# 512-column products in four more kinds of stage, weights stored in blocks, and a convolution tap on ScalarE

## What is computed

```
# block 1
h = rms_norm(x, pre_mix_g);  z = h @ w_in                      # 2048 x 4096: q, k, v, u
m = concat(chunked_attention(q, k, v), multiscale_pool(u)) @ w_o   # "mixer output"
x = x + rms_norm(m, post_mix_g)
h = rms_norm(x, pre_ffn_g)
up = causal_dwconv(h @ w_up, conv_w, conv_b)                   # 3 taps along the sequence
y = (gelu(up[:, :5632]) * up[:, 5632:]) @ w_down               # down projection
x = x + rms_norm(y, post_ffn_g)
# block 2: adaptive norms from 64 column blocks of w_ada, two attentions, a gated merge, a SwiGLU
kv = modulate(norm(ctx and x)) @ w_in_2[:, :3072];  q = modulate(norm(x)) @ w_in_2[:, 3072:6144]
gates = modulate(norm(x)) @ w_in_2[:, 6144:]
x = x + gate * ((sigmoid(ga) * (oa @ w_br_a) + sigmoid(gb) * (ob @ w_br_b)) @ w_out)
x = x + gate * ((silu(h @ w_ff_gate) * (h @ w_ff_up)) @ w_ff_down)
```

## Time and profile before

| | |
|---|---|
| median of 3 runs | 3146.78 us (3143.88 to 3147.21) |
| the profiled execution | 3145.76 us |
| its span, first to last instruction | 3143.9 us |
| mean granted TensorE clock | 0.970 |
| TensorE busy | 2926.2 us (93%) |
| VectorE / ScalarE / GpSimd busy | 1946.6 / 1564.1 / 786.3 us |
| HBM read | 594.99 MB, 190 GB/s over the span |

### The profile page before, as it was taken

One profiled execution on the slowest core, in us unless ns is written; L12 is line 12 of the kernel. 1 busy time (PEld: TensorE's weight loads), 2 busy tenths in 40 slices (PEclk: granted clock), 3 DMA queues, 4 the chain that ended last, 5 costly groups with the idle time before them and its releaser, 6 DMA issues.

```text
span 3143.9 us, 57610 instructions
## 1 busy us (share of the span) xinstructions
PE 2926.2 (93%) x20282; PEld 2699.2 (86%) x20282; DVE 1946.6 (62%) x2412; ACT 1564.1 (50%) x2203; POOL 786.3 (25%) x646
## 2 busy tenths in 40 slices
PE   7998789999998997999998778999997999999999
PEld 7988789999988997788898547999996888888888
DVE  5566888776688866433456555655766665555554
ACT  5555554345565543323455645665535644334443
POOL 2554432003233321212341402445303400000000
PEclk9999899999999998999998989999998999999999
DMA  7874666657777764344574003887755865656655
GB/s 245 266 246 126 222 201 201 180 181 243 240 225 227 235 218 148 120 149 135 180 248 140 1 1 125 255 261 247 241 182 178 255 213 181 188 186 187 187 185 163
DMA packets 595176, 598.29 MB, mean 190 GB/s; under 512 B 18257, under 2 KB 593105, under 8 KB 594833
## 3 DMA queue, kind: packets, MB, share of 16 engines
q1 hardware_dynamic: 591936, 589.37, 60.3%
q10 hardware_dynamic: 2368, 4.91, 0.4%
q0 software_dynamic: 784, 2.88, 0.3%
HBM read 594.99 MB, written 2.10 MB: 190 GB/s over the span
## 4 chain that ended last, share of the span: by engine, by line
PE 60%; DVE 15%; DMA 10%; ACT 7%; issue 7%; DVEq 1%; ACTq 0%; SPq 0%
PE acc L1334 19%; PE acc L1330 13%; PE acc L1332 13%; PE acc L1333 12%; DVE wlo L850 5%; DMA raw<-w_ada 5%; DMA raw<-w_in 2%; ACT whi L540 2%; ACT cond_products L536 1%; DVE cond_sums L842 1%; DVE conv_out L936 1%; PE sums L1392 1%; DMA raw<-w_up 1%; DMA raw<-w_brb 1%; DVE conv_in L924 1%
## 5 line engine op out<-in xcount | busy, mean ns | idle before, releaser
L850 DVE TENSOR_TENSOR wlo<-raw,whi 128x1024 fp32r<-128x1024 f32 x864 | 1120.3, 1307 | 892.5 <-ACT whi L540 888.9
L1334 PE MATMUL acc<-operand,wlo 128*128 128x256 f32 (+1 forms) x5504 | 1606.6, 292 | 0.0
L540 ACT ACTIVATE whi<-raw 128x1024 fp32r<-128x1024 f32 x864 | 911.3, 1058 | 1096.5 <-PE acc L1334 733.5
L1332 PE MATMUL acc<-operand,whi 128*128 128x256 f32 (+1 forms) x4096 | 1222.6, 298 | 98.3 <-DVE wlo L850 63.4
L1333 PE MATMUL acc<-operand,whi 128*128 128x256 f32 (+1 forms) x4096 | 1210.7, 296 | 0.0
L1334 PEld LDWEIGHTS acc<-operand,wlo 128*128 128x128 f32 x5504 | 1063.0, 193 | 15.4
L1332 PEld LDWEIGHTS acc<-operand,whi 128*128 128x128 f32 x4096 | 795.4, 194 | 125.4 <-DVE wlo L850 56.5
L1333 PEld LDWEIGHTS acc<-operand,whi 128*128 128x128 f32 x4096 | 795.6, 194 | 15.0
L408 POOL TENSOR_TENSOR cond_products<-cond_products 128x512 f32<-128x512 f32 x192 | 252.6, 1316 | 1425.9 <-ACT cond_products L536 1424.0
L1330 PE MATMUL acc<-operand,whi 128*128 128x512 f32 x1408 | 502.9, 402 | 16.9 <-DVE wlo L850 9.0
L536 ACT ACTIVATE cond_products<-raw,cond_silu 128x256 f32<-128x256 f32 x768 | 327.8, 498 | 255.7 <-PE acc L1334 159.3
(11 more groups left out here) (201 smaller groups left out, 2000.0 us busy)
## 6 DMA issues: line engine op xcount, KB each, us to landing
raw<-w_ada SPq DMA_DIRECT2D x256, 512.0 KB, 4.7
raw<-w_in SPq DMA_DIRECT2D x224, 512.0 KB, 4.8
raw<-w_up SPq DMA_DIRECT2D x176, 512.0 KB, 4.8
raw<-w_down SPq DMA_DIRECT2D x88, 512.0 KB, 4.9
raw<-w_fg SPq DMA_DIRECT2D x88, 512.0 KB, 4.3
raw<-w_fu SPq DMA_DIRECT2D x88, 512.0 KB, 4.5
raw<-w_fd SPq DMA_DIRECT2D x88, 512.0 KB, 3.5
raw<-w_o SPq DMA_DIRECT2D x32, 512.0 KB, 4.8
```

Of the source, the lines that this page charges most:

```text
L540: act.activation(whi[j % RING][:], raw[j % RING][:], ACT.Copy).then_inc(hi_done, 2 if st.entries[j % st.upb - 1] == (None, ADA_VEC) else 1)
L850: dve.tensor_tensor(wlo[j % RING][:], raw[j % RING][:], whi[j % RING][:].bitcast(F32), ALU.subtract).then_inc(lo_done, 2 if prev[0] is Non ...
L1332: pe.matmul(out_, h[:, x, f], mov[:, 0], start=first, stop=False)
L1334: ins = pe.matmul(out_, l[:, x, f], mov[:, 0], start=False, stop=last)
```

## The change

- **Block layout.** Each of the eleven weight matrices is rearranged on the host to [partition, column block, row tile, 256 columns]; a unit is then 128 rows of 4 KB, one for each partition. For a partition the distance to the next is a 128th of the matrix, 128 KB (w_o) to 768 KB (w_ada).
- **512-column products** in kinds mix_out, down1, down2 and q too. In three of them (LOW_FIRST) ScalarE first copies the low half's sums from PSUM to the result tile (`low_half`), and VectorE's evacuation, which now comes after `lo`, adds the other half instead of copying. In down2 VectorE adds both halves.
- **Convolution.** VectorE's `evac` keeps only L924. The newest tap with the bias is made by ScalarE (`newest_tap`, two ACTIVATE Identity, right behind the `hi` of that step). VectorE makes the older taps in a function of its own, after `lo`: for the first group after the `lo` of the next ring entry, for the second after the `lo` of the same step, ahead of `finish`.

```diff
-V_STEPS = {"scale": 0, "mix_out": 3, "conv": (6, 9), "down1": 0, "down2": 3, "kv": 0, "q": 0, "gate": 0,
+V_STEPS = {"scale": 0, "mix_out": 3, "conv": (4, 7), "down1": 0, "down2": 4, "kv": 0, "q": 0, "gate": 0,
            "branch_a": 0, "branch_b": 1, "out": 4, "glu": (0, 3), "down_x": 3}
-A_STEPS = {"conv": (1, 0), "gate": (1, 1), "glu": (2, 1)}
-WIDE = ("glu", "down_x")
+A_STEPS = {"conv": (2, 1), "gate": (1, 1), "glu": (2, 1), "mix_out": 1, "down1": 1, "q": 1}
+WIDE = ("glu", "down_x", "mix_out", "down1", "down2", "q")
+LOW_FIRST = ("mix_out", "down1", "q")
...
+    def block_of(w, g, k):
+        return W[w][:, ds(g, 1), k:k + UK, :].rearrange("p g k c -> p (g k) c")
     def cols(w, k, c0, stride):
-        return lambda b, GB, gb, u: W[w][:, k + UK * u:k + UK * u + UK, ds((b * GB + gb) * stride + c0, GW)]
+        return lambda b, GB, gb, u: block_of(w, (b * GB + gb) * (stride // GW) + c0 // GW, k + UK * u)
...
...
             def post(st, b, gb):
                 g = group(st, b, gb)
-                if st.kind == "conv" and gb % 2 == 0:
+                if st.kind == "conv":
                     act.wait_ge(evac_done, g + 3)
                     act.activation(Gb[:], Cb[:], ACT.Gelu_apprx_tanh).then_inc(astep, 1)
...
+            def low_half(st, b, gb):
+                tile = b * (2 * st.GB) + (st.tile0 + 2 * gb)
+                act.wait_ge(used, grouped(st, b, gb))
+                act.activation(R[:, ds(tile if st.kind == "q" else tile + Yt, 2), :], PS[:, gb % 2, :, S:2 * S],
+                               ACT.Copy).then_inc(astep, 1)
...
+            def newest_tap(st, b, gb):
+                act.wait_ge(vstep, vst(st, b, gb, 0))
+                t2 = b * 2 + (FT * (gb % 2) + st.feat0 + VEC["conv_w"] + 4 * FT)
+                tb = b * 2 + (FT * (gb % 2) + st.feat0 + VEC["conv_b"])
+                for m in range(2):
+                    ins = act.activation(Cb[:, m, :], Zp[:, m, 2:S + 2], ACT.Identity, scale=V[:, ds(t2 + m, 1)],
+                                         bias=V[:, ds(tb + m, 1)])
+                ins.then_inc(astep, 1)
...
-                    at = j - RING - (2 if st.kind == "conv" else 0)
-                    if at in st.last:
+                    at = j - RING
+                    if st.kind == "conv":
+                        if at in st.last:
+                            newest_tap(st, b, st.last.index(at))
+                        elif at - 2 == st.last[0]:
+                            post(st, b, 0)
+                    elif at in st.last and st.kind in LOW_FIRST:
+                        low_half(st, b, st.last.index(at))
+                    elif at in st.last:
                         post(st, b, st.last.index(at))
...
-                if k == "q":
-                    dve.tensor_copy(R[:, ds(tile, 2), :], sums).then_inc(evac_done, 1)
-                elif k == "down1":
-                    dve.tensor_copy(R[:, ds(tile + Yt, 2), :], sums).then_inc(evac_done, 1)
+                if k in ("q", "down1"):
+                    y = R[:, ds(tile + Yt if k == "down1" else tile, 2), :]
+                    dve.wait_ge(astep, ast(st, b, gb, 0))
+                    dve.tensor_tensor(y, sums, y, ALU.add).then_inc(evac_done, 1)
...
                 elif k == "mix_out":
                     y = R[:, ds(tile + Yt, 2), :]
-                    did(dve.tensor_copy(y, sums))
+                    dve.wait_ge(astep, ast(st, b, gb, 0))
+                    did(dve.tensor_tensor(y, sums, y, ALU.add))
...
                         did(dve.tensor_tensor(y, y, sums, ALU.add))
+                        settled()
+                        did(dve.tensor_tensor(y, y, low, ALU.add))
...
                         did(dve.tensor_tensor(Zp[:, :, 2:S + 2], sums, rep(RS[:], 2), ALU.mult))
-                        settled()
...
-                        if gb % 2:
-                            dve.wait_ge(astep, ast(st, b, 0, 0))
-                        for m in range(2):
-                            did(dve.tensor_scalar(Cb[:, m, :], Zp[:, m, 2:S + 2], V[:, ds(t0 + (4 * FT + m), 1)],
-                                                  V[:, ds(tb + m, 1)], ALU.mult, ALU.add))
...
+            def older_taps(st, b, gb):
+                did, settled = steps_from(st, b, gb, 1)
+                settled()
+                dve.wait_ge(astep, ast(st, b, gb, 0))
+                t0 = b * 2 + (FT * (gb % 2) + st.feat0 + VEC["conv_w"])
+                for tap in (1, 0):
+                    for m in range(2):
+                        if tap == 0:
+                            settled(2)
+                        ins = dve.scalar_tensor_tensor(
+                            out=Cb[:, m, :], in0=Zp[:, m, tap:S + tap], scalar=V[:, ds(t0 + (2 * FT * tap + m), 1)],
+                            in1=Cb[:, m, :], op0=ALU.mult, op1=ALU.add)
...
-                    gate = st.kind in ("gate", "glu")
+                    gate = st.kind in ("gate", "glu", *LOW_FIRST)
...
                     if gb is not None and gate:
                         evac(st, b, gb)
+                    if st.kind == "conv" and gb != 0 and (gb == 1 or j - RING == st.last[0] + 1):
+                        older_taps(st, b, gb or 0)
                     if gb is not None:
                         finish(st, b, gb)
...
+    by_block = lambda w: np.ascontiguousarray(
+        w.reshape(w.shape[0] // P, P, w.shape[1] // GW, GW).transpose(1, 2, 0, 3))
...
-        "w_o": a["w_o"][0], "w_up": a["w_up"][0], "w_down": a["w_down"][0], "w_ada": a["w_ada_2"][0],
+        "w_o": by_block(a["w_o"][0]), "w_up": by_block(a["w_up"][0]), "w_down": by_block(a["w_down"][0]),
...
```

More of the change, by code:

```diff
@@ L125, in build @@
           w_fg, w_fu, w_fd, out):
-    km = lambda w: w.rearrange("(k p) n -> p k n", p=P)
-    W = {k: km(v) for k, v in dict(w_in=w_in, w_o=w_o, w_up=w_up, w_down=w_down, w_in2=w_in2, bra=w_bra, brb=w_brb,
-                                   out=w_out2, fg=w_fg, fu=w_fu, fd=w_fd).items()}
-    ada_src = km(w_ada)
+    W = dict(w_in=w_in, w_o=w_o, w_up=w_up, w_down=w_down, w_in2=w_in2, bra=w_bra, brb=w_brb, out=w_out2, fg=w_fg,
+             fu=w_fu, fd=w_fd, ada=w_ada)
+    def block_of(w, g, k):
+        return W[w][:, ds(g, 1), k:k + UK, :].rearrange("p g k c -> p (g k) c")
     def cols(w, k, c0, stride):
-        return lambda b, GB, gb, u: W[w][:, k + UK * u:k + UK * u + UK, ds((b * GB + gb) * stride + c0, GW)]
+        return lambda b, GB, gb, u: block_of(w, (b * GB + gb) * (stride // GW) + c0 // GW, k + UK * u)
     def pairs(wg, wu, g0, u0):
-        return lambda b, GB, gb, u: W[(wg, wu)[gb % 2]][:, UK * u:UK * u + UK,
-                                                          ds(b * GW + (g0, u0)[gb % 2], GW)]
+        return lambda b, GB, gb, u: block_of((wg, wu)[gb % 2], b + (g0, u0)[gb % 2] // GW, UK * u)
     h1c = FIRST_HALF // 2 * GW
@@ L364, in load @@
                     if gb is None:
-                        src = ada_src[:, UK * u:UK * u + UK,
-                                      ds((b + st.ib) * GW - (ADA_CTX * GW if st.ib >= ADA_CTX else 0), GW)]
+                        src = block_of("ada", b + (st.ib - (ADA_CTX if st.ib >= ADA_CTX else 0)), UK * u)
                     else:
@@ L870, in evac @@
                 sums = PS[:, gb % 2, :, 0:S]
+                low = PS[:, gb % 2, :, S:2 * S]
                 tile = b * (2 * st.GB) + (st.tile0 + 2 * gb)
@@ L948, in evac @@
                         did(dve.tensor_tensor(Gb[:], Cb[:], Gb[:], ALU.mult))
+            def older_taps(st, b, gb):
[10 more added lines that the diff above has]
+                            in1=Cb[:, m, :], op0=ALU.mult, op1=ALU.add)
+                        if gb % 2 == 0 and tap == 0 and m == 1:
+                            ins.then_inc(evac_done, 1)
+                        else:
+                            did(ins)
             def finish(st, b, gb):
@@ L955, in finish @@
                     src = X[:, ds(tile, 2), :] if k == "out" else R[:, ds(tile + Yt, 2), :]
-                    did, settled = steps_from(st, b, gb, 2 if k == "out" else 1)
+                    did, settled = steps_from(st, b, gb, 1 if k == "mix_out" else 2)
                     settled()
@@ L964, in finish @@
                     val = Cb if k == "conv" else Gb
-                    did, settled = steps_from(st, b, gb, 7 if k == "conv" else 2)
+                    did, settled = steps_from(st, b, gb, 5 if k == "conv" else 2)
                     settled()
```

21 lines of the change are left out of this document (4 added, 17 removed).

## The result

The changed kernel takes 3104.97 us (median of 4, 3100.55 to 3120.01) against 3145.33 us for the kernel before (4 runs, 3136.34 to 3147.21): ratio 0.9886, 95% interval 0.9847 to 0.9924. It is faster, and inside the range, but by 40 us and not by 66. The profiled execution spans 3103.5 us (before 3143.9).

What follows compares the result with a forecast made beforehand. TensorE, busy 93% of the span, was taken to bound the kernel, with waits mainly in conv bodies with conditions. Savings of 7.2 + 22.2 + 36.6 = 66 us off 3145.76 gave 3080 us, range 3050 to 3123.

Steps and rivals of the forecast that it cites:

- D: Rival, chance 0.05: the far row pitch lengthens landings in 46 three-load bodies; with 1 us more, 3259 us.
- C: Rival, chance 0.13: landings do not shorten, non-conv stages stay, convolution gets about half its gain; 3121 us.
- B: Rival, chance 0.2: conv bodies gain nothing, as older taps behind a subtraction hold back Gelu and splits; 3116 us.
- A: Rival, chance 0.17: conv bodies reach TensorE's floor of 23.5 us, gaining 57.6 instead of 36.6 us; 3059 us.
- products: In down1, down2 and the queries, 512-column products save 0.053 us in each of 136 units: 7.2 us.
- the bodies that were to come near their floor: w_in, mix_out, gates, branches, glu1a: shorter landings bring bodies near TensorE's own pace, 22.2 us in sum.
- convolution: Bodies of up2 and up1a shorten to 25.0 us, gaining 24.3 and 12.3, together 36.6 us.
- the steps from E: Conv body, from the start of the first group's L924: subtraction to E+4.1, older taps to E+7.2, then Gelu.
- I take 26.5 - 1.5 = 25.0: Conv bodies with conditions fall to 25.0 us, TensorE waiting some 1.5 us a body instead of 3 to 5.
- so it lies in idle time: ScalarE's low-half copy, 0.58 us a group in mix_out, down1 and q, costs nothing; without that cover 16 us.
- 0.4 to 0.8: Block layout: fall in us of a load's landing in bodies with conditions, 4.8 to about 4.0; 0.8 taken.
- The step from 19.4 to 24.9 GB/s an engine: Block layout: longer pieces move faster, so a 512 KB load takes all engines 1.31 us instead of 1.69.

Runs made afterwards that it cites:

- conv_only: The kernel before with only the convolution's edits, row layout and narrow products kept: 3111.83 us, ratio 0.9900.
- the second pair of executions: The changed kernel and the kernel before, each once more with nothing edited: 3096.79 and 3130.85 us.
- layout_only: The kernel before with the block layout and nothing else: 3135.96 us, ratio 0.9976.
- mix_narrow: The changed kernel with the mixer output back at 256-column products and its old evacuation: 3097.87 us, ratio 0.9852.
- no_layout: The changed kernel with the weights stored row by row as before: 3117.90 us, ratio 0.9918.
- context_later: tap_later with POOL's load of the second block's context issued after GpSimd's part of the norm: 3089.78 us, ratio 0.9833.
- mix_evac_late: context_later with 512-column products in the mixer output again, its first evacuation and norm sums behind a subtraction: 3101.51 us, ratio 0.9850.
- changed_again: The changed kernel once more, nothing edited: 3096.79 us.
- mix_by_vector: The changed kernel with VectorE, not ScalarE, taking the low half in the mixer output: 3106.58 us, ratio 0.9879.
- tap_later: mix_narrow with ScalarE's first newest tap one step later, behind the next weight unit's split: 3092.68 us, ratio 0.9825.

## Why the prediction was right, and where its sizes were off

**Direction, mechanism and range were right.** Order and tap make up2's bodies shorter, the pieces at 1.2 GHz are gone, and no rival decided: not D (landings fell), not C (w_in and the gates did come to their floor), not B (the bodies gained), not A (they stayed 2.5 us above the floor). conv_only against the kernel before shows that the convolution carries the gain. The range was met better than the forecast: 40 us lie between the forecast's 66 and the 29 and 25 of B and C, and 9 of them are the pace of the execution, which the prediction didn't know of. Without those, 31 us, the total alone could not have told the forecast from B or C; the bodies and landings do.

Term by term, in the two profiled executions: products 7.2 us forecast and about 10.6 measured; the bodies that were to come near their floor 22.2 and 6.0 (w_in 2.6, gates 4.6, glu1 2.0 that is pace, branches -0.4, mixer output -2.8); convolution 36.6 and 14.0; the pace of the plain stages nothing and 9.0.

**The term that was mis-sized most is the convolution**, 36.6 us forecast, 14.0 measured (-12.6 in up2, -1.4 in up1; the second pair of executions gives -14.1 and -4.6). In up2 the steps from E were nearly right. VectorE in one body after:
```profile
947.75 0.68 DVE L952 TENSOR_TENSOR conv_in<-acc,rstd 128x512 f32<-128x512 f32 x1
950.83 1.46 DVE L875 TENSOR_TENSOR wlo<-raw,whi 128x1024 fp32r<-128x1024 f32 x1 [2.39 <-ACT whi L541]
952.21 2.14 DVE L969 SCALAR_TENSOR_TENSOR conv_out<-conv_in,vectors,conv_out 128x256 f32<-128x256 f32 x4
954.28 1.21 DVE L875 TENSOR_TENSOR wlo<-raw,whi 128x1024 fp32r<-128x1024 f32 x1
956.00 1.23 DVE L875 TENSOR_TENSOR wlo<-raw,whi 128x1024 fp32r<-128x1024 f32 x1 [0.51 <-ACT whi L541]
958.62 1.50 DVE L875 TENSOR_TENSOR wlo<-raw,whi 128x1024 fp32r<-128x1024 f32 x1 [1.39 <-ACT whi L541]
```
The subtraction ends at E+4.5 (forecast E+4.1) and the older taps at E+6.6 (forecast E+7.2, with the 3.16 us of the earlier trace rows, which GpSimd's work beside them had stretched; here 2.14). What failed is the last step, "I take 26.5 - 1.5 = 25.0". VectorE's work did fall to 20.98 us, but it stands idle for the other 5.0, of which 4.3 are the three waits for ScalarE above. Chain by line of this body:
```profile
by line: DMA raw<-w_up 36.1%; issue 27.7%; ACT whi L541 15.6%; ACT cond_products L537 9.8%; DVE wlo L875 7.7%; DVE conv_out L969 6.5%; ACT L537 4.9%; ACT conv_out L577 4.4%; DVE conv_in L952 2.6%; ACTq L620 0.5%; DVEq L969 0.5%; DVEq L873 0
```
Landings and ScalarE's split, product and tap stand where VectorE stood. It is the chain of load, split and subtraction that held w_in before, now with the tap and the Gelu in ScalarE's fixed order. I had looked for slack on VectorE, and the gain ended where the ring's chain came next. ScalarE's order in that body also holds something that the walk left out:
```profile
952.63 1.28 ACT L549 ACT_TABLE_LOAD   x1
954.38 0.63 ACT L549 ACTIVATE gate_act<-conv_out 128x512 f32<-128x512 f32 x1 [0.47 <-DVE conv_out L969]
...
962.00 1.28 ACT L537 ACT_TABLE_LOAD   x1
963.30 1.71 ACT L537 ACTIVATE cond_products<-raw,cond_silu 128x256 f32<-128x256 f32 x4
```
A body has two such table loads of 1.28 us, one ahead of the Gelu and one ahead of a later product of the condition; the kernel before has as many, 55 in the whole execution. The second is on the chain above (ACT L537, 4.9% of 25.98 us). The first stands, with the Gelu and four products, between the splits that start at 951.55 and 957.47, and VectorE waits 1.39 us for the latter. What the table loads cost a body is not shown: every kernel here has them.

**up1** has the same gain per body as far as its starts show ((489.26 - 411.82)/3 = 25.81 against 28.07, 2.3 us), some 7 us over three bodies. It was given back ahead of them: 57.2 us instead of 50.5 from the first load of w_up to the first repeated body. That stretch holds the end of the mixer output, the norm and the context's load. conv_only has 51.4 there, layout_only 54.9, mix_narrow 55.1 and no_layout 58.1: the layout alone adds 3.5 us, the wide mixer output alone 6.7, both together no more than that, so the two don't add up. With the context's load moved away context_later is back at 51.5. With the context's load at its old place, SP's pair of weight loads right behind it takes 7.5 to 9.8 us in the kernels in which ScalarE copies the mixer output's low half, and 2.7 to 3.3 in the others. That the loads collide in time is argued from these numbers, not measured by itself.

**Mixer output: wrong sign.** The step that failed is "so it lies in idle time". The copy's engine was idle on average; at the copy's place in ScalarE's order it was not, and VectorE's evacuation and norm, with a subtraction behind them, inherited the delay. If VectorE takes the low half, the block ahead of that subtraction grows by an addition of 0.7 us, and more of it falls beside GpSimd's sums: both forms make it 5.0 us instead of 3.4. Even with the block out of the way wide products gained nothing here (mix_evac_late).

**Layout.** The landing fell by 0.4 us, the lower end of "0.4 to 0.8". The step from 19.4 to 24.9 GB/s an engine failed: 589.37 MB in 60.3% of 16 engines' 3103.5 us are 19.7, so the few loads of the earlier trace rows were no guide to a full queue. The 0.4 us sufficed for w_in and the gates. The ten executions with blocks have bodies of 23.3 to 23.6 us in w_in and 23.6 to 23.8 in the gates, the four executions with rows 23.6 to 24.0 and 24.0 to 24.4. One body of w_in after, TensorE's from end to end:
```profile
by line: PE acc L1361 33.6%; PE acc L1363 32.5%; PE acc L1362 32.5%; PE ada_sums L1372 1.4%
```
branch_a's bodies came to 23.5 us (forecast 23.6). A branch_b body went from 24.07 to 25.34, but it varies: 23.5 to 24.7 in the executions with rows, 23.7 to 26.1 in those with blocks. glu1a stayed at (2486.17 - 2363.08)/5 = 24.62 (forecast 23.3), 23.82 in changed_again. The chain of one of its bodies after; its largest part is still a landing:
```profile
by line: DMA raw<-w_ada 40.5%; issue 15.9%; ACT whi L541 11.8%; DVE wlo L875 11.0%; ACT cond_products L537 7.7%; ACT L537 5.1%; PE acc L1359 4.8%; ACT gate_act L569 2.5%; ACT gate_act L557 2.3%; PE acc L1363 1.9%; ACT L569 1.9%; ACTq L530 0
```

The Trainium skill, "DMA: Bandwidth & Descriptors", section "Latency and other measured facts", lets copies slow down with a large power-of-two row pitch; at the pitches here the landings got shorter, 4.8 to 4.4 us, with an unchanged share of the engines. Pitch and length of the pieces changed together, so no run here shows either alone.

**Products.** down1 -3.7 and down2 -2.2 against 2.5 and 2.1 forecast. The pace of the execution doesn't enter here: mix_by_vector ran at the slower pace and takes 142.7 us in down1, the changed kernel at the faster one 142.6, and the kernel before 146.3 and 146.2 at the two paces. Over all fourteen executions the wide kernels have 142.3 to 145.2 and 110.4 to 113.0 us in the two stages, the narrow ones 145.8 to 146.7 and 114.7 to 115.4. In the queries a body went from 25.27 us to 24.48, and takes 24.4 to 24.6 in every wide kernel at either pace: 4.7 us over six bodies against 2.5 forecast. So the width earned about 10.6 us where 7.2 were forecast, and lost some 2 in the mixer output.

**Left open:** what sets the pace of an execution; whether and why the shorter landing lengthens the old convolution's bodies and those of branch_b; and which of load, split, tap, table load and Gelu holds a convolution body at 25.6. tap_later showed that the place of the first tap is worth 0.3 us of it, no more.

## What to carry to other kernels

An engine that is busy on average half the time is no cover for an instruction that another engine waits for: look at what stands ahead of it in its own order, and at what stands behind the waiting one. In a ring of buffers, work that nobody waits for goes behind the instruction that frees the next buffer; in up2's bodies that order was worth twice as much as moving the work to another engine. Even so it has to be tried: in the mixer output the same move took back only what the wide products had cost. And when an engine is relieved, price the chain that comes next (landing, split, subtraction) before taking the whole relief as a gain.

## What the runs showed of the hardware

- The same stream of 512- and 256-column products ran at 2.827 us a unit in one execution and at 2.773 in another of the same program, the same in all plain stages of an execution, at a granted clock of 1.00 in both. Over these kernels that is 9 us and some 2 more in glu1b, a quarter of the effect that was to be measured. Stretches of 256-column products (up1b, 23.04 us a body) and the stages with conditions don't show it.
- A 512 KB load in 4 KB pieces holds the DMA engines about as long as one in 1 KB pieces (19.7 and 19.4 GB/s an engine). Only its landing (4.8 to 4.4 us) is shorter, and SP's issue (0.37 to 0.33).
- VectorE's older taps and subtractions, which read SBUF tiles, took longer only where GpSimd worked beside them. Of the older taps in the changed kernel's execution, 128x256, all 153 that overlap no GpSimd instruction take 0.47 to 0.49 us; the 23 that overlap one take 0.955 in the middle. For the subtraction of 128x1024 it is 1.15 to 1.23 us (560 of them) against 1.48 (304, up to 3.27). Without an overlap none of either passes 0.49 and 1.23 us in any of the fourteen executions. L952, which reads the sums from PSUM, stays at 0.68 to 0.69 either way. A block's length can't be had from one row of each; it depends on what GpSimd does in that moment.
- A table load of ScalarE took 1.28 us each time, 55 times in an execution.
